# A two-layer encoder kernel: the attention heads' chain one scan step earlier with its diagonal matrices made by GpSimd, sines made two steps ahead, scan outputs taken by ScalarE but for one product, output matrices loaded unpadded

## The reference, cut to what matters

```
h = rmsnorm(x, g_mix[i]);  z = h @ w_in[i];  u, q, k, v = split(z)
y_ssm: states = associative_scan(lam_bar, b_bar u) forward and backward
       y = Re(C states) + D u;  y = gelu(y);  y = y * sigmoid(y @ w_glu + b_glu);  rmsnorm
y_att: softmax(q1 k1 + bias) - lam * softmax(q2 k2 + bias), times v, per-head rmsnorm
x = x + concat(y_ssm, y_att) @ w_out[i]
x = x + swiglu(rmsnorm(x))          # layer 0: dense, layer 1: top-2-of-8 experts
```

## Time and profile before

| | us |
|---|---|
| median of 3 runs | 1429.87 (1426.37 to 1430.4) |
| profiled execution, its own time | 1424.49 |
| its span in the trace | 1422.7 |
| PE busy | 1337.5 (94%) |
| DVE busy | 852.9 (60%) |
| ACT busy | 679.5 (48%) |
| POOL busy | 134.3 (9%) |

### The profile page before, as it was taken

One profiled execution on the slowest core, in us unless ns is written; L12 is line 12 of the kernel. 1 busy time (PEld: TensorE's weight loads), 2 busy tenths in 40 slices (PEclk: granted clock), 3 DMA queues, 4 the chain that ended last, 5 costly groups with the idle time before them and its releaser, 6 DMA issues.

```text
span 1422.7 us, 18990 instructions
## 1 busy us (share of the span) xinstructions
PE 1337.5 (94%) x7246; PEld 970.9 (68%) x7246; DVE 852.9 (60%) x1095; ACT 679.5 (48%) x991; POOL 134.3 (9%) x111
## 2 busy tenths in 40 slices
PE   6996889999899888999999999999999999999996
PEld 5865558888787654876667676766766666666663
DVE  6868654454397875665554756555655555665552
ACT  6358443434274763344444544454544444444442
POOL 0356100000006640000000000000000000000000
PEclk9898999999999999999999999999999999999999
DMA  8352335453643236699999999999999999999994
GB/s 339 96 219 80 124 131 194 178 177 118 257 143 119 68 119 261 253 421 387 409 420 421 421 421 421 410 420 422 420 421 421 410 420 421 421 421 421 420 422 179
DMA packets 66328, 435.57 MB, mean 306 GB/s; under 512 B 8192, under 2 KB 14720, under 8 KB 16576
## 3 DMA queue, kind: packets, MB, share of 16 engines
q1 hardware_dynamic: 64848, 429.60, 75.1%
q0 software_dynamic: 1392, 4.78, 0.9%
HBM read 429.11 MB, written 2.10 MB: 303 GB/s over the span
## 4 chain that ended last, share of the span: by engine, by line
PE 74%; DVE 9%; DMA 8%; ACT 5%; SPq 2%; issue 1%; ACTq 0%; DVEq 0%
PE ps L2249 19%; PE ps L2284 11%; PE ps L2235 9%; PE ps L2138 8%; DMA raw<-wmoe 6%; PE ps L2266 6%; PE ps L2117 4%; PE ps L1902 3%; PE ps L2043 2%; PE ps L2058 2%; DMA first_ring<-wmoe 2%; PE ps L2020 2%; SPq L567 2%; PE ps L1943 1%; PE ps L2031 1%
## 5 line engine op out<-in xcount | busy, mean ns | idle before, releaser
L2138 PE MATMUL ps<-wsplit,xh 128*128 128x512 f32 (+1 forms) x352 | 112.6, 391 | 4.9 <-DVE hv L1429 3.3
L1439 DVE TENSOR_TENSOR low_raw<-raw,last_uppers 128x2048 fp32r<-128x2048 f32 x39 | 89.1, 2289 | 39.1 <-ACT last_uppers L869 39.1
L1439 DVE TENSOR_TENSOR low_first<-first_ring,first_uppers 128x2048 fp32r<-128x2048 f32 x31 | 70.8, 2291 | 37.6 <-ACT first_uppers L869 37.5
L1902 PE MATMUL ps<-hT,mixw 128*128 128x256 f32 x384 | 90.4, 398 | 2.6 <-DMA mixw<-wmix 1.6
L2284 PE MATMUL ps<-raw,hn 128*64 128x256 f32 x784 | 92.4, 382 | 0.0
L1439 DVE TENSOR_TENSOR low_raw<-raw,first_uppers 128x2048 fp32r<-128x2048 f32 x31 | 70.8, 2289 | 32.2 <-ACT first_uppers L869 32.2
L1403 DVE TENSOR_TENSOR wsplit<-raw,wsplit 128x2048 fp32r<-128x2048 f32 x33 | 74.5, 2289 | 20.1 <-ACT wsplit L828 20.1
L1902 PEld LDWEIGHTS ps<-hT,mixw 128*128 128x128 f32 x384 | 76.2, 200 | 15.2 <-issue 2.2
L1707 DVE TENSOR_TENSOR hv<-hv,ps 128x256 f32<-128x256 f32 x56 | 23.6, 421 | 103.8 <-ACT hv L1028 103.8
L2284 PE MATMUL ps<-last_ring,hn 128*64 128x256 f32 x704 | 83.2, 382 | 0.0
L1028 ACT ACTIVATE hv<-ps 128x256 f32<-128x256 f32 x56 | 21.5, 384 | 127.5 <-PE ps L2249 127.5
(11 more groups left out here) (367 smaller groups left out, 2930.1 us busy)
## 6 DMA issues: line engine op xcount, KB each, us to landing
raw<-wmoe SPq DMA_DIRECT2D x148, 1024.0 KB, 22.4
first_ring<-wmoe SPq DMA_DIRECT2D x95, 1024.0 KB, 23.2
last_ring<-wmoe SPq DMA_DIRECT2D x91, 1024.0 KB, 23.4
raw<-wdense SPq DMA_DIRECT2D x33, 1024.0 KB, 5.0
mixw<-wmix SPq DMA_DIRECT2D x12, 2048.0 KB, 8.3
cyt<-bmat SPq DMA_DIRECT2D x2, 2048.0 KB, 12.1
cw<-cmat SPq DMA_DIRECT2D x2, 2048.0 KB, 18.3
qk<-wglu SPq DMA_DIRECT2D x2, 1024.0 KB, 4.9
```

Source lines behind the costliest of these rows:

```text
L1439: tt(lows[at], ring[at], uppers[k % UPPERS].bitcast(F32), ALU.subtract).then_inc(s["lo_done"], 1)
L1902: ins = mm(ps[:, bank(u), j * 256:j * 256 + 256], mixw[:, c % 2, f, n * P:(n + 1) * P], hT[:, f, :], start=(f == 0), stop=(f == KT - 1))
L2138: ins = mm(to, x2[:, fx, t * P:(t + 1) * P], of, start=(fx == 0 and i == 0), stop=(fx == KT - 1 and i == 2))
```

## The change

1. **The head chain.** `T_DIAG` goes from 3 to 2, `T_TURN` from 4 to 3, `T_OUT` from 5 to 4. The diagonals are no longer four ScalarE instructions but one GpSimd instruction of the same 512 elements, which stands in GpSimd's stream behind its three instructions of that step. The eviction `AT` gets a semaphore of its own, and ScalarE does `AT` of one head ahead of the next head's exponentials. `oms`, `atn` and the GLU move one step earlier with it.
2. **Sines.** Four buffers instead of three; ScalarE makes them two steps ahead. The wait on GpSimd's products names the same step of GpSimd as before.
3. **take_y and gelu_in.** ScalarE makes the square, the copy and 1 + 0.044715 y² (one instruction more); VectorE does one product, which reads `y_sum` in PSUM. TensorE's next write of that bank waits for VectorE's product (`gin`).
4. **Output matrices.** 0.5 MB a layer without the zeros come into a sine buffer; `fold_c` makes 4 instructions of 1024 elements and 4 more on 64 partitions each, which write into a `cw` that GpSimd has set to zero (a memset of 4096 elements a partition, at the start and at the end of the dense feed-forward).
5. The scratch rows `small` move into sine buffer 3, so `trigs(1)` waits for `fold_c`.

```diff
-T_EXP, T_SUMS, T_DIAG, T_TURN, T_OUT = 1, 2, 3, 4, 5
+T_EXP, T_SUMS, T_DIAG, T_TURN, T_OUT = 1, 2, 2, 3, 4
+TRIGS = 4
@@ beside
-            work.append((f"turn{h}", "A"))
+            work.append((f"turn{h}", "T"))
@@ sync engine
-                sp.dma_start(cw[:], cmat[l]).then_inc(s["in_c"], 16)
+                sp.dma_start(sines[:, 1:3], cmat[l]).then_inc(s["in_c"], 16)
@@ gpsimd
+                if l:
+                    pool.wait_ge(s["piece_done"], 3 * NC_D)
+                nc.gpsimd.memset(cw[:], 0.0).then_inc(s["cw_zero"], 1)
                 for i in range(GP):
...
+                    for h in range(HEADS):
+                        if i == HEAD_AT[h] + T_DIAG:
+                            pool.wait_ge(s["sums_ready"], HEADS * l + h + 1)
+                            pool.wait_ge(s["unit_done"], unit(l, f"turn{h - 1}" if h else "zqkv5") + 1)
...
+                            nc.gpsimd.tensor_tensor(diag.rearrange("p m q t -> p (m q) t"), ones_at, weights,
+                                                    ALU.mult).then_inc(s["diag_ready"], 1)
@@ trigs
-                if n >= 3:
-                    act.wait_ge(s["products"], n - 2)
+                if n >= TRIGS:
+                    act.wait_ge(s["products"], n - TRIGS + 1)
@@ take_y
                 act.wait_ge(s["c_done"], GP * l + 4 * (ft + 1))
+                chain[0] += 1
+                nc.scalar.activation(th[:, ft], y_sum, ACT.Square).then_inc(s["act_chain"], 1)
                 nc.scalar.activation(yt[:, ft], y_sum, ACT.Copy)
-                nc.scalar.activation(th[:, ft], y_sum, ACT.Square).then_inc(s["y_taken"], 1)
+                act.wait_ge(s["act_chain"], chain[0])
+                nc.scalar.activation(th[:, ft], th[:, ft], ACT.Copy, bias=1.0, scale=0.044715).then_inc(s["y_taken"], 1)
@@ scalar engine, attention
-                elif at == T_DIAG:
-                    act.wait_ge(s["sums_ready"], HEADS * l + h + 1)
...
-                            ins = nc.scalar.activation(diag[:, m, q], ident, ACT.Copy, scale=col[:, c:c + 1])
-                    ins.then_inc(s["diag_ready"], 1)
@@ scalar engine, steps
                 trigs(l, 0)
+                act.wait_ge(s["cw_ready"], l + 1)
+                trigs(l, 1)
                 for i in range(STEPS):
-                    if i + 1 < GP:
-                        trigs(l, i + 1)
+                    if i + 2 < GP:
+                        trigs(l, i + 2)
...
-                    for at in (T_EXP, T_DIAG, T_TURN, T_OUT):
+                    for at in (T_TURN, T_EXP, T_OUT):
@@ fold_c
+                for k in range(2):
+                    for r in range(2):
+                        ins = tt(ctmp[:, 2 * k + r], c(r), f(k), ALU.mult)
+                link(ins)
+                dve.wait_ge(s["cw_zero"], l + 1)
+                for g in range(2):
...
+                    tt(to[:, 0], ctmp[at, 0], ctmp[at, 3], ALU.subtract)
+                    ins = stt(to[:, 1], ctmp[at, 1], -1.0, ctmp[at, 2], ALU.mult, ALU.subtract)
@@ gelu_in
-                link(stt(th[:, ft], th[:, ft], 0.044715, yt[:, ft], ALU.mult, ALU.mult))
-                tt(th[:, ft], th[:, ft], yt[:, ft], ALU.add).then_inc(s["gin"], 1)
+                tt(th[:, ft], th[:, ft], y_sum, ALU.mult).then_inc(s["gin"], 1)
@@ outputs
                 if i % 4 == 0 and FT * l + ft:
-                    pe.wait_ge(s["y_taken"], FT * l + ft)
+                    pe.wait_ge(s["gin"], FT * l + ft)
```

More of the change, by code:

```diff
@@ L325, in encoder @@
         late = sb("late", [P, 5, SEQ])
-        trig = sb("trig", [P, 3, 3, SEQ])
+        sines = sb("sines", [P, TRIGS, 2, SEQ])
+        cosines = sb("cosines", [P, TRIGS, SEQ])
         ush = sb("ush", [P, PAIRS, NCH + 1])
         usw = sb("usw", [P, PAIRS, NCH])
-        small = sb("small", [P, 20, ST])
+        kept = sb("kept", [P, 2, ST])
         fold = sb("fold", [P, 2, 2 * ST])
@@ L462, in at_least, with row @@
                 eng.wait_ge(s[what], n)
+        passing = sines[:, 3].rearrange("p d (r n) -> p (d r) n", n=ST)
+        turn_rate, decay_rate = kept[:, 0], kept[:, 1]
+        csrc = sines[:, 1:3].rearrange("p b d (i n) -> p b (d i) n", n=GROUP)
+        def row(r, n=1):
+            at = r - 1 if r > 4 else r
+            return passing[:, at:at + n] if n > 1 else passing[:, at]
         def turn_part(i):
@@ L801, in attention @@
                         ins.then_inc(s["emptied_act"], 1)
-                elif at == T_DIAG:
-                    act.wait_ge(s["sums_ready"], HEADS * l + h + 1)
-                    if h:
-                        full(unit(l, f"turn{h - 1}"))
-                    for m in range(2):
-                        for q in range(TT):
-                            c = 80 + 4 * (h % 2) + 2 * m + q
-                            ins = nc.scalar.activation(diag[:, m, q], ident, ACT.Copy, scale=col[:, c:c + 1])
-                    ins.then_inc(s["diag_ready"], 1)
-                elif at == T_TURN:
+                if at == T_TURN:
                     u = unit(l, f"turn{h}")
@@ L1227, in scalars @@
                 lre, lim = pr[:, Q_LRE:Q_LRE + ST], pr[:, Q_LIM:Q_LIM + ST]
-                tt(sm[:, 9], sm[:, 3], sm[:, 6], ALU.mult)
-                link(tt(sm[:, 10], sm[:, 3], sm[:, 5], ALU.mult))
+                tt(row(9), row(3), row(6), ALU.mult)
+                link(tt(row(10), row(3), row(5), ALU.mult))
                 def by(r):
-                    return sm[:, r].rearrange("p (i d) -> p i d", d=2)
+                    return row(r).rearrange("p (i d) -> p i d", d=2)
                 def own(k):
@@ L1268, in lam @@
                 def lam(r, d):
-                    return (small[:, r].rearrange("p (k a d h) -> p k a d h", a=2, d=2, h=1)[:, :, :, d, :]
+                    return (row(r).rearrange("p (k a d h) -> p k a d h", a=2, d=2, h=1)[:, :, :, d, :]
                             .to_broadcast([P, PAIRS, 2, 32]))
@@ L1336, in rotate_in @@
                 bu = ps[:, scan_bank(n)].rearrange("p (r t) -> p r t", r=2)
[L1337 removed]
+                tt(ri2[:], bu[:, ::-1, :], sines[:, n % TRIGS], ALU.mult).then_inc(s["bu_read"], 1)
                 dve.wait_ge(s["bu_read"], n + 1)
[L1339 removed]
+                tt(bu, bu, cosines[:, n % TRIGS:n % TRIGS + 1, :].to_broadcast([P, 2, SEQ]), ALU.mult).then_inc(s["bu_turned"], 1)
             def add_in(l, i):
@@ L1866, in free @@
                     who, n = emptied(u - RINGN)
-                    pe.wait_ge(s["emptied_act" if who == "A" else "emptied_dve"], n)
+                    pe.wait_ge(s[EMPTIED[who]], n)
             def empty_wait(u):
                 who, n = emptied(u)
-                pe.wait_ge(s["emptied_act" if who == "A" else "emptied_dve"], n)
+                pe.wait_ge(s[EMPTIED[who]], n)
             def norm(l):
```

109 lines of the change are left out of this document (54 added, 55 removed).

## The result

The changed kernel takes 1465.28 us (median of 3 runs, 1459.13 to 1470.08) against 1429.87: ratio 1.0248, 95% interval 1.0208 to 1.0288. The forecast was 1469 with a range of 1440 to 1487. The profiled execution took 1459.13 us, its span is 1457.3, that is 34.6 more than before.

The account below looks back on a forecast made before the run. The experts' weight stream, released by routing, was taken as the bound, so mixer delays go through one for one. Terms summed to +40.7 us on the profiled 1424.5, so 1465.2, given as 1469 for the median; range 1440 to 1487.

Parts of the forecast that it names:

- What bounds the kernel: Experts' weights stream at a full DMA queue once routing releases it, so mixer time goes through one for one.
- Output matrices and clock in layer 0: Before `local`: shorter `fold_c` gains 0.9 us a layer; without the pause layer 0 keeps its clock, -5.6 us.
- The head chain: In the mixers: a closed ring of waits makes three `turn` periods 42.7 us against 30.0, +12.7 a layer.
- The clock at `turn`: Idle TensorE ahead of `turn` drops the clock, 1.73 us each for three of four a layer: +10.4, bounds 0 and 13.8.
- Last `turn` to last `outputs`: End of the head chain in each mixer: 11.6 us instead of 9.2, +2.4 a layer.
- Last `outputs` to the projection: End of each mixer: the last `gelu_out` stands behind the second `head_norm`; 24.1 us against 21.2, +2.9 a layer.
- The memset: Start of layer 1: GpSimd's 3.8 us memset holds up VectorE's scaling of the norm, +1.7 us, bounds 0 and 8.
- The sum: Whole kernel: all terms together +40.7 us on the profiled 1424.5, so 1465.2; given as 1469 for the median.
- The signs: Rows to show it right: `turn` 14 to 16 us apart, named waits, last `outputs` 12 to 20 us later, `local` near 7.4.
- rival "faster": Mixers: the ring does not decide, GpSimd's own period of 10.7 us does; 1414.5 us, chance 0.08.
- the ring: Mixer waits: GpSimd's three instructions, diagonals, `turn`, `AT`, exponentials, `map`, `outputs`, back to GpSimd; 14.4 us a period.

Follow-up runs that it names:

- `gelu_out` run: Changed kernel with the last gelu_out moved ahead of the second head_norm on VectorE; median 1460.0 us, 1.0215 of before.
- late memset: Changed kernel with GpSimd's memset of layer 1 held back until just ahead of fold_c; median 1464.6 us, 1.0250 of before.
- run with matmuls ahead of `turn`: Changed kernel with eight unneeded matmuls added ahead of each turn in TensorE's idle time; median 1452.5 us, 1.0175 of before.
- run with the sines back: Changed kernel with the head chain as before and sines again made one step ahead; median 1419.7 us, 0.9943 of before.

## Why the prediction was right

- **What bounds the kernel.** A microsecond in a mixer goes through to the end: 34.5 of stretches make 34.6 of span. Right, though the queue was full from the eighteenth slice and not from the sixteenth, as I read it.
- **Output matrices and clock in layer 0**, forecast -0.9 and -5.6: measured -7.2 to the first `turn`. `fold_c` took 9.4 us against the 9.2 forecast. Right, though no run has this part alone. Layer 1 gained 2.9 instead of 0.9, of which 2.2 stand in its first projection, 14.05 us against 16.24, which is clock and not this edit.
- **The head chain**, forecast 14.4 a period at the high clock, +12.7 a layer: right in its links and their order. (The links as listed add up to 14.5; that is 0.3 a layer.) The diagonals took 1.04 us (1.26 forecast, the lower bound 1.0); the warm period measured 14.14. Two runs bear out who closes the ring: the diagonals taken off GpSimd's queue took 41 us off the time, the exponentials ahead of `AT` 18.
- **The clock at `turn`**, forecast +10.4 for six cold `turn`: right that it counts, wrong in what it touches. `turn` took 2.8 to 3.8 us, about 1.1 more than warm in the middle of the chain, not always 1.73; but `map` and `outputs` run behind it at the same low level, 4.72 us where I had put 3.15 with the handoff. The first two periods were 17.0 to 17.7 instead of my 16.1. The third was 13.4 and 13.5 instead of 15.6: with `map` out of it, `outputs` ran warm again. Three periods so came to 48.05 and 47.43 us against the 47.9 forecast. That they agree so well is luck: an error of about +2 and one of -2 cancel. In slower executions the first two periods were longer still (18.0 to 18.3 in the profile of the `gelu_out` run, which took 1466.8 us).
- **Last `turn` to last `outputs`**, forecast +2.4: measured +4.1, since I left the fourth `turn` warm, and it took 3.75 us.
- **Last `outputs` to the projection**, forecast +2.9: measured +1.7. The gather behind `head_norm` is what TensorE waits for in layer 0 (1.30 us), but the output products at the low clock end at nearly the same moment, which I had not seen; in layer 1 they alone set the time. So the cause I gave held in part, and the term was too large by 1.2 a layer.
- **The memset**, forecast +1.7: measured +1.9, its length 3.51 us against 3.8. I had put the scaling itself behind the memset; in the trace it is the tiny instructions ahead of the scaling that wait. By the rule of the Trainium skill that I had named ("SBUF — State Buffer", Who interferes with whom), a VectorE instruction in a two-port mode is blocked until GpSimd's has ended; the trace agrees, 2.30 us for a copy of two elements that ended with the memset.
- **The sum** was 40.7 against 34.6. The periods came out 1.6 us under the forecast (34.2 against 35.8), of which 1.3 is that I had taken layer 1's 30.0 us for layer 0 as well, where the kernel before had 31.3. The front was 3 us better, the end 1 us worse; 3.1 us came back in stretches that the change doesn't touch (the dense part and the projection of layer 1), where only the clock differs.
- **The signs.** Those that named who waits for whom all came: about 4.0 us of idle ahead of three `turn` of four, the waits of L834, L2006 and the reciprocal, none of L1364 for sines, the last gather behind L1414, `local` at 7.36 us in layer 0. Two numbers missed: the `turn` rows lay 17.0, 17.0 and 13.5 us apart in layer 1 and not 14 to 16, and the last `outputs` came 21.0 and 21.4 us later against the first `turn`, not 12 to 20.
- **The rival "faster"** named the point from which it would decide, 3.9 us over `turn`, `AT`, the exponentials and `map`. It needed one more condition that I had not seen: with the exponentials ahead, `head` takes their place in the ring, and the period stays at 13.4 instead of 10.7.

## What to carry to other kernels

Before an instruction is given to an engine that has room, ask what that engine waits for: GpSimd was busy 10% of the time, and the diagonals cost 41 us there because they stood behind products that waited for the matmuls that waited for them. Two edits that look harmless met here. The eviction ahead of the exponentials cost nothing against the kernel before as long as ScalarE made the diagonals (1424.1 us); the diagonals on GpSimd cost 20 us even with the exponentials first (1447.0), since `head` closed the ring in their place. Walk the wait of each moved instruction around all engines until it comes back or ends, and when one link is taken out, look for what stands next to it in the queue.

## What the runs showed of the hardware

- The runs of one kernel spread with their clock. Over the comparisons the kernel before ran from 1416.0 us at a mean granted clock of 0.981 to 1434.0 at 0.970, and all of its 47 runs there lie within 4 us of the line between these two: 18 us for 0.011. The changed kernel's three runs go the same way, 1459.1 us at 0.965 to 1470.1 at 0.960. A difference of a few microseconds between two profiles can be no more than this.
- GpSimd holds VectorE up by the kinds of the two instructions, not by their size. A copy of two elements took 2.30 us beside the memset; four `tensor_tensor` of 1024 elements beside the same memset took 4.62 us, as without it. But beside GpSimd's own `tensor_tensor` a tiny one of VectorE was held, in the run with the exponentials first:

```profile
489.01 1.27 POOL L682 TENSOR_TENSOR raw<-raw,cosines 128x512 f32<-128x512 f32 x1
489.13 1.17 DVE L1406 TENSOR_TENSOR col<-col 128x2 f32<-128x2 f32 x1
```

It took 1.17 us and ended with GpSimd's, where it takes 0.16 alone. The Trainium skill ("SBUF — State Buffer", Who interferes with whom) has this too: a VectorE instruction with two inputs in SBUF contends with a GpSimd instruction that reads SBUF, not with one that only writes it. The traces agree in both pairs with two inputs, the tiny one held beside GpSimd's products and the four products free beside the memset; by this rule the late memset costs `fold_c` nothing. The copy that was held beside the same memset has one input and falls under the rule on two-port modes named above.
- The low clock outlasts the first matmuls behind an idle time. The windows of the changed kernel's ring in layer 1, columns as above:

```profile
494.40:497.50 3.10, 3.10 (x16) 2.81 (x16) 0.00 (x0) 0.00 (x0) 3.02 (x3) 0.61 0.00 0
...
502.00:505.00 3.00, 3.00 (x14) 1.73 (x13) 2.90 (x7) 2.97 (x7) 0.00 (x0) 0.50 0.02 5
505.00:507.30 2.30, 2.30 (x33) 1.95 (x32) 2.27 (x6) 1.46 (x5) 0.94 (x1) 0.93 0.01 4
```

`turn` ran mostly at the low level, `map` wholly, and only `outputs` and `bu_pair` had the clock back. The same matmuls behind 0.3 us of idle ran at 1.00 in the run with matmuls ahead of `turn`, in its period of 14.14 us. The length of the idle time alone did not decide: behind 2.54 us a `turn` took 2.02 us in the kernel before, behind 2.55 us one took 3.38 in the run with the sines back.
